# Half of the fourth expert's first weights in X's place while the experts run

## What is computed

```python
for i in range(2):
    h = mixer_ab(x) if i == 0 else mixer_c(x)             # two different mixers
    x = layer_norm(ALPHA * x + h)
    m = hierarchical_moe(x, ...)                          # below
    x = layer_norm(ALPHA * x + m)
    x = x + sigmoid(x @ ple_w_gate[i]) * (p[i] @ ple_w_proj[i])

def hierarchical_moe(x, ...):       # 4 groups of 8 experts; each row goes to 2 experts of its best group
    h = xt[tok] @ w_gu[e]                                 # w_gu[e]: 1024 x 1024, 4 MB
    a, b = split(h, 2)
    y[tok] += gate * ((silu(a) * b) @ w_down[e])          # w_down[e]: 512 x 1024, 2 MB
```

## Time and profile before

| | us |
|---|---|
| median of 3 runs (1575.98 to 1578.79) | 1576.2 |
| the profiled execution's own time | 1575.88 |
| its span in the trace | 1574.0 |
| TensorE busy | 1393.9 (89%) |

### The profile page before, as it was taken

The page is one execution under the profiler, slowest core; times in us unless marked ns, Lnnn a source line. Parts: engine busy times, 40 slices in busy tenths (PEclk is TensorE's granted clock), DMA queues, the critical chain, the costliest instruction groups (busy, mean ns, idle before and its releaser), DMA issues. The chain is left out here.

```text
span 1574.0 us, 18121 instructions
## 1 busy us (share of the span) xinstructions
PE 1393.9 (89%) x6544; PEld 736.2 (47%) x6544; DVE 458.4 (29%) x1108; ACT 357.7 (23%) x726; POOL 243.9 (15%) x370
## 2 busy tenths in 40 slices
PE   8997999988787888879999999899887878889897
PEld 7885883332222333325768657743322222333246
DVE  4445360000000100019769563610000000101085
ACT  4124021111010110114546781211110111101141
POOL 0004011111111111110003461011111111111100
PEclk9999979999999999999999999989999999999998
DMA  8130759999999999994511004689999999999951
GB/s 298 54 134 7 305 225 392 427 429 428 430 427 430 428 429 428 425 374 166 190 40 54 1 2 177 270 360 422 431 427 430 428 429 430 427 429 428 383 217 54
DMA packets 79367, 482.64 MB, mean 307 GB/s; under 512 B 18432, under 2 KB 20484, under 8 KB 46536
## 3 DMA queue, kind: packets, MB, share of 16 engines
q1 hardware_dynamic: 68632, 463.85, 71.2%
q0 software_dynamic: 10240, 16.82, 2.8%
q10 hardware_dynamic: 432, 1.11, 0.2%
HBM read 474.91 MB, written 23.59 MB: 317 GB/s over the span
## 5 line engine op out<-in xcount | busy, mean ns | idle before, releaser
L1002 PE MATMUL PS<-wide,w 128*64 128x512 f32 x1984 | 450.3, 603 | 47.7 <-ACT w L1021 29.0
L1016 PE MATMUL PS<-slim,w 128*64 128x512 f32 x992 | 252.9, 656 | 80.7 <-issue 79.0
L1002 PEld LDWEIGHTS PS<-wide,w 128*64 128x64 f32 x1984 | 137.2, 138 | 329.0 <-issue 261.1
L1016 PEld LDWEIGHTS PS<-slim,w 128*64 128x64 f32 x992 | 84.7, 149 | 242.9 <-issue 240.5
L1028 DVE TENSOR_TENSOR w<-w,PS 128x256 f32<-128x256 f32 x64 | 27.0, 421 | 535.5 <-ACT w L1025 535.5
L1025 ACT ACTIVATE w<-PS 128x256 f32<-128x256 f32 x64 | 24.6, 384 | 502.2 <-PE PS L1002 502.2
L1031 DVE COPY w<-PS 128x256 f32<-128x256 f32 x64 | 27.2, 425 | 299.8 <-PE PS L1009 299.8
L1806 ACT ACTIVATE w<-PS,w 128x512 f32<-128x512 f32 x62 | 42.6, 688 | 315.2 <-PE PS L1016 315.2
L1673 POOL COPY w<-w 128x1 uint32 (+1 forms) x62 | 11.3, 183 | 657.7 <-ACT w L1806 657.7
L975 POOL DMA_INDIRECT w<-x_rows,w x64 | 67.7, 1058 | 71.6 <-POOL w L1666 51.0
L981 POOL DMA_INDIRECT y_rows<-w x62 | 63.5, 1024 | 55.1 <-POOL w L1673 53.9
(11 more groups left out here) (312 smaller groups left out, 1950.0 us busy)
## 6 DMA issues: line engine op xcount, KB each, us to landing
wide<-in_moe_w_gu SPq DMA_DIRECT2D x124, 2048.0 KB, 25.5
slim<-in_moe_w_down SPq DMA_DIRECT2D x62, 2048.0 KB, 25.5
w<-in_moe_w_gu SPq DMA_DIRECT2D x4, 2048.0 KB, 11.7
wide<-in_ple_w_gate SPq DMA_DIRECT2D x4, 2048.0 KB, 14.4
w<-in_ab_w_in SPq DMA_DIRECT2D x2, 2048.0 KB, 12.7
w_in<-in_ab_w_in SPq DMA_DIRECT2D x2, 2048.0 KB, 9.4
out_raw<-in_ab_w_out SPq DMA_DIRECT2D x2, 2048.0 KB, 11.2
XT<-in_moe_w_down SPq DMA_DIRECT2D x2, 2048.0 KB, 10.1
```

The lines of the kernel that those rows point to most:

```text
L1002: m = pe.matmul(PS[u * SLOTS:(u + 1) * SLOTS, 2 + q, :], xeT[q][:, k, :], gu[k].rearrange("p (a u c) -> p a u c", a=2, u=2)[:, :, u, :], s ...
L1016: m = pe.matmul(PS[u * SLOTS:(u + 1) * SLOTS, 6 + q, :], gT[:, k, :], dn[k][:, u * NB:(u + 1) * NB], start=(k == 0), stop=(k == FF // P - 1))
```

## The change

In each layer half 0 of expert 3's first weights (2 MB) no longer goes into the `wide` tile of area 0, but into `X`, which nothing else needs between the end of the router's turns and the Injection. It comes in four loads of 512 KB, one per tile of X, by SP's queue: tiles 0 and 1 behind the store of tile 1 to `x_rows` (after a wait for the stores' landing and for the turns to have read X), tile 2 behind the loads that follow the products, tile 3 behind the wait for the gathers. Area 0's half 0 so takes expert 5's half 0 at once, in the place in the queue where expert 3's was; expert 5's half 1 keeps its place; the queue between is 2 MB shorter. Behind the last expert's down weights SP reads X back from `x_rows` in four loads of 512 KB, ahead of `Y0` and `Y1`. VectorE and TensorE wait for 48 instead of 32 on the semaphore of each tile (X besides `Y0` and `Y1`). The semaphore of the stores of X is split in two (SP's and ACT's), and three semaphores of the first stage are given back to make room.

```diff
+        def load_stead(eng, l, t):
+            w = A["moe_w_gu"][l, STEAD, 0:NB, :].rearrange("(p c) n -> p c n", p=P)
+            eng.dma_start(X[:, t, :], w[:, t, :]).then_inc(stead_in[l], 16)
...
+            def load_stead_behind(sp, first, end):
+                sp.wait_ge(s_rows[0], 16 * end)
+                turn.wait(sp, end - 1)
+                for t in range(first, end):
+                    load_stead(sp, l, t)
...
                     for t in range(T - 1):
                         sp.wait_ge(norm.done, t + 1)
-                        sp.dma_start(x_rows[t * P:(t + 1) * P, :], X[:, t, :]).then_inc(s_rows, 16)
+                        sp.dma_start(x_rows[t * P:(t + 1) * P, :], X[:, t, :]).then_inc(s_rows[0], 16)
+                        if t == 1:
+                            load_stead_behind(sp, 0, 2)
                     sums.wait_full(sp, 2 * T - 1)
                     load_after_products(sp)
+                    load_stead_behind(sp, 2, 3)
...
                 for q in range(2):
                     sp.wait_ge(s_gath[q], 16)
+                load_stead(sp, l, T - 1)
...
-                pool.wait_ge(s_rows_in[l], 16 * T)
+                pool.wait_ge(s_rows_in[l][0], 16 * (T - 1))
+                pool.wait_ge(s_rows_in[l][1], 16)
...
                     if t == ADDED_BY_PE:
-                        pe.wait_ge(self.s_y[t], 32)
+                        pe.wait_ge(self.s_y[t], 48)
...
-                        dve.wait_ge(self.s_y[t], 32)
+                        dve.wait_ge(self.s_y[t], 48)
...
-                    gu_after(0, 3, 0, 1)
+                    wait_alone(sp, s_gu_half[0], 1, sp_tick)
+                    load_gu(sp, l, 0, 5, halves=(0,))
+                    wait_alone(sp, s_gu[0], 1, sp_tick)
+                    load_gu(sp, l, 0, STEAD, halves=(1,))
                     gu_after(1, 4, 1, 1)
                     dn_after(0, 3, 0, 1)
                     dn_after(1, 4, 1, 1)
-                    gu_after(0, 5, 1, 2)
+                    wait_alone(sp, s_gu[1], 2, sp_tick)
+                    load_gu(sp, l, 0, 5, halves=(1,))
...
                     dn_after(0, LAST, 1, PAIRS - 1)
+                    for t in range(T):
+                        sp.dma_start(X[:, t, :], x_rows[t * P:(t + 1) * P, :]).then_inc(inj.s_y[t], 16)
...
+                        stead = isinstance(i, int) and expert(q, i) == STEAD
+                        gu = third_gu if a is None else [X[:, k, :] for k in range(T)] + gu_of[0][T:] if stead else gu_of[a]
...
+                            elif stead and half == 0:
+                                pe.wait_ge(stead_in[l], 16 * T)
                             else:
-                                pe.wait_ge(gu_in[l][a][half], 16 * loads + 16)
-                            gate_up(pe, q, third_gu if a is None else gu_of[a], half).then_inc(done[q], 1)
+                                fewer = 1 if half == 0 and q == 1 and a == 0 else 0
+                                pe.wait_ge(gu_in[l][a][half], 16 * (loads - fewer) + 16)
+                            gate_up(pe, q, gu, half).then_inc(done[q], 1)
```

More of the change, by code:

```diff
@@ L246, in build @@
         s_ln = lasting("s_ln")
-        s_gain = lasting("s_gain")
-        s_dec = lasting("s_dec")
-        s_pool = lasting("s_pool")
+        s_gain = nc.alloc_semaphore("s_gain")
+        s_dec = nc.alloc_semaphore("s_dec")
+        s_pool = nc.alloc_semaphore("s_pool")
         QT, KT = three(w1[:, 0:2048], SEQ), three(w1[:, 2048:4096], SEQ)
@@ L471, in build @@
         dn_in = [[lasting(f"dn_in{l}{q}") for q in range(2)] for l in range(2)]
+        stead_in = [lasting(f"stead_in{l}") for l in range(2)]
+        STEAD = 3
         def load_gu(eng, l, q, e, halves=(0, 1)):
@@ L632, in build @@
         Stages.end()
+        Stages.now.extend([s_gain, s_dec, s_pool])
         def route_views():
@@ L690, in build @@
         LG_ALL = PS[:, 0:2 * T:2, 0:NG + NE]
-        s_rows_in = [lasting(f"rows_in{l}") for l in range(2)]
+        s_rows_in = [[lasting(f"rows_in{l}"), lasting(f"last_rows_in{l}")] for l in range(2)]
         def out_projection(l, products, w_sems, load_first, load_half_way, load_after_products):
@@ L765, in _ @@
                     act.wait_ge(norm.done, T)
-                    act.dma_start(x_rows[(T - 1) * P:T * P, :], X[:, T - 1, :]).then_inc(s_rows, 16)
+                    act.dma_start(x_rows[(T - 1) * P:T * P, :], X[:, T - 1, :]).then_inc(s_rows[1], 16)
                 @block.sync
```

## The result

The changed kernel took 1588.72 us (median; 1588.16 to 1590.28), the kernel before 1577.49 on the same chip (1575.98 to 1579.66): a ratio of 1.0089, 95% interval 1.0074 to 1.0104. The profiled execution spans 1586.8 us, against 1574.0 before. The forecast of no change was wrong, and the time lies outside its range.

What follows compares the result with a forecast made beforehand. In the experts' DMA plateaus bytes were taken to set the time. Layer 0's +0.1 us and layer 1's -0.2 gave -0.1 on 1575.88; with the median 0.3 above, 1576.0 us was forecast, range 1573.0 to 1581.0 (8 in 10).

Steps and rivals of the forecast that it cites:

- The rest: Outside the changed loads: other products and norms untouched, one more subtraction in TensorE's loop lying under waits for loads.
- Its last part: Signs to check; if right, VectorE's first addition or `mix(1)` waits for `Y`, TensorE idle 2 to 4 us behind `mix(0)`.
- X's way back: Behind the last down weights: X and `Y` of tiles 0 and 1, eight loads at 1.25 us each, 10.0 us.
- The first rival: Slower: the eight 512 KB loads ahead of `mix(1)` take 1.68 us each, 6.7 us in all, 1582.9; chance 0.11.
- The landing of `Y` in layer 0: End of layer 0: X and the `Y` of tiles 0 and 1 land 10.0 us behind the last weights, at 707.6.
- The faster rival: Faster: X's way back is hidden by idle DMA engines, 2.2 and 3.5 us reach the end, 1570.5; chance 0.12.
- The gain of the early weights: In the experts: the shorter queue lands the last down weights 2.2 us earlier in layer 0, 3.5 in layer 1.
- the gap isn't repeated: Behind expert 5's half 1: the next load still finds 1.5 MB of side loads, 3.7 us, ahead, so no second gap.
- The comparison in layer 0: End of layer 0: `mix(1)`, begun at 707.5 before, now waits for `Y` at 707.6, so +0.1 us.
- Loads ahead of the gathers: X's tiles 0 to 2, 1.5 MB or 3.7 us, cost nothing; tile 2's store lands some 2.4 us later, under cover.
- The gate weights ... they'd be next to be late: Behind `Y`: the gate weights come later by 5.0 - 2.2 us in layer 0 and would be next to be late.
- The one with the empty queue: Slower: the shorter queue saves nothing, `Y` late by X's whole length, +2.3 and +3.3 us, 1581.8; chance 0.06.

Runs made afterwards that it cites:

- e9_fill14: Changed kernel with 14 products of nothing in TensorE's order between `mix(0)` and `mix(1)`: 1576.95 us, ratio 1.0020 to the kernel before.
- e12_before_gate: Kernel before with the second half of the gate weights moved ahead of tile 3's `Y`, X left alone: 1574.75 us, ratio 1.0004.
- e2_no_way_back: Changed kernel without the four loads that bring X back, waits set back to 32: 1573.58 us, ratio 0.9990 to the kernel before.
- e8_split: Changed kernel with only X's tile 0 reloaded ahead of `Y`, tile 1 behind its `Y` for VectorE alone, tiles 2 and 3 ahead of theirs: 1578.61 us, ratio 1.0035.
- e5_both: Changed kernel with X's tiles 2 and 3 reloaded right ahead of their own `Y`, plus 6 filler products ahead of `mix(1)`: 1577.18 us, ratio 1.0027.
- e4_interleave: Changed kernel with X's tiles 2 and 3 reloaded right ahead of their own `Y`: 1577.80 us, ratio 1.0024 to the kernel before.
- e11_both_gates: `Y` and X order of the changed kernel with TensorE awaiting five loads, gate weights moved ahead of tiles 2 and 3's X and `Y`: 1576.97 us, ratio 1.0018.

## Why the prediction was wrong, step by step

**The step that failed** is in "The rest": "The other products and norms are untouched". They are untouched in the code, but `mix(1)` and `mix(2)` took 12.2 and 9.9 us instead of 6.9 and 7.0: 8.2 of the 12.4 us. The prediction had the cause in its hands. Its last part says that TensorE would idle 2 to 4 us behind `mix(0)`, and it measured 3.99 and 3.90. It took that idle time for cover, since `mix(1)` would begin when it used to, and didn't ask what clock TensorE would have afterwards. That e9_fill14, with the same landings, has neither the low clock nor the longer products shows it. The rest of the miss is 1.7 us of gain that was missing and the 2.4 us of routers and first store. The Trainium skill has the rule: "TensorE: Matmul & The Clock Gate", section "HAM oscillation — how this bites in real kernels", says that TensorE, left idle long enough by a wait for a DMA between two groups of products, starts the next group at half clock. The trace agrees: 0.51 granted behind the wait, 2.07 us for two products instead of 1.12.

**X's way back, right.** Eight loads in 10.1 us in both layers, 10.0 forecast; 1.26 each, 1.25 forecast. The first rival, loads at 1.68, is wrong. The Trainium skill's rule ("DMA: Bandwidth & Descriptors", section "Bandwidth") would have made them 1.63 as an estimate, with the 75% that the page gives for 1 MiB or more. Measured behind other loads they show nothing of it. The landing of `Y` in layer 0, forecast for 707.6, was 706.9. In layer 1 `mix(1)` came 9.8 us behind its forecast: 8.5 of these were there at the first gather (1032.05 against 1023.55 us), from layer 0's end and layer 1's router, and 1.2 are the smaller gain. The faster rival, X through idle DMA engines, is out with this: `Y` landed the full eight loads behind the weights.

**The gain of the early weights, mis-sized.** Counted from the first gather (227.06 and 1032.05 us after, 228.30 and 1023.55 before), expert 5's half 1 landed 2.7 us earlier in layer 0 (275.95 + 7.7 against the earlier trace rows; 2.2 forecast) and 3.8 in layer 1 (3.5 forecast); it took 7.7 and 7.8 us from its issue, 8.2 forecast. But "the gap isn't repeated" was wrong. Layer 1's next load was issued 59.2 us behind the gather as before, its place having come free no sooner (the row at 1091.30), and landed only 2.7 us earlier; in layer 0 the gain fell to 2.3 at that load and to 1.4 two loads later. At the end of the experts 1.7 and 2.3 us were left, 1.7 less in sum than the 5.7 forecast.

**The comparison in layer 0, lucky.** The 707.5 us at which `mix(1)` began before (707.3 in the trace) was itself late: the clock of the earlier trace rows is 0.66. In e12_before_gate, with the same loads ahead of `mix(1)` and no low clock there, it begins 5.8 us behind the weights, not 7.5. What the prediction took for the expert's own late chain was in part a low clock, and it hid 1.7 us of the way back.

**Loads ahead of the gathers, right.** Both first gathers are released by VectorE's list as before, and e2_no_way_back has no loss:

```profile
227.06 1.21 POOL L997 DMA_INDIRECT w<-x_rows,w  x1 [9.42 <-DVE w L971]
...
1032.05 1.13 POOL L997 DMA_INDIRECT w<-x_rows,w  x1 [9.88 <-DVE w L971]
```

Tile 2's store landed 6.7 us behind its issue instead of 2.6, so 4.0 us later and not 2.4; the cover held. Layer 1's router took 3.6 us more, layer 0's 2.2 less, and that is the clock again. In all 28 routers of the fourteen traces the time goes with how long the clock was low between the first store and the first gather: 35.8 to 36.7 us with 4.3 us or less of it, 38.2 to 38.4 with 10.2 to 11.1, 39.8 to 39.9 with 13.9 to 14.1. The kernel before has 10.5 and 0.2 us of it, the changed one 4.3 and 14.0. The early loads don't seem to decide which: the nine traces with them have routers of 37.4 us (layer 0) and 38.1 (layer 1) on average, the five without 37.8 and 37.4. So I don't book these to the change. That the low clock of layer 0's end moved them is possible and wasn't tried.

**"The gate weights ... they'd be next to be late", right**, and it mattered only when the first wait was gone: 2.90 us in e8_split, 1.21 in e5_both. In the changed kernel itself TensorE was too late to notice.

**The rivals.** The one with the empty queue had X's length unhidden, which is what `mix(1)` shows, counted from the landing of the weights (+2.5 and +3.3), but not for its reason: the gain was there, though smaller. No rival had the clock, and so none came near 1588.7.

## What to carry to other kernels

A wait that begins early enough to end "on time" isn't free: price what TensorE runs behind it at half clock, or put products into it. Where loads stand in one line, an added one delays each thing behind it, so write down the slack of every item (here 1.0 us for the gate weights) and move what has slack behind what has none. When a wait is taken away, the next item in that line is what the time shows.

## What the runs showed of the hardware

- Of the 28 layer ends traced, nine have a wait of 0.90 to 6.58 us ahead of `mix(1)`, and in all nine the clock fell in the wait or behind it: behind 1.64, 1.35 and 0.90 us too (e4_interleave, e11_both_gates). Of the nineteen with 0.70 us or less it fell in one, behind 0.51 (e11_both_gates), and not behind 0.70 (e9_fill14) or 0.57 (the kernel before). The length of the idle time alone doesn't decide; the low stretches at such waits lasted 3.4 to 13.7 us, not in proportion to it.
- Over fourteen traces routers that compute the same took 35.8 to 39.9 us, by how long the clock was low in them; in a kernel with such stretches a difference of 2 or 3 us in one stage of one trace is no evidence until the clock in it is read.
- Loads of 512 KB that stand ready behind others took 1.26 us each, eight in a row at a DMA share of 1.0 and 403 to 416 GB/s.
